# Query and key weights of an mLSTM head multiplied into one block projection, and the first head's row terms fed by two early loads

## The reference, cut to what matters

```
q = _headwise(xc, w_q)          # each group of 4 channels times its own 4 x 4 block
k = _headwise(xc, w_k)
v = _headwise(xm, w_v)
...
s = einsum('bhtd,bhsd->bhts', qc, kc) * exp(d - m_t)         # scores between tokens t and s
num = a * einsum('bhtd,bhdv->bhtv', qc, C) + einsum('bhts,bhsv->bhtv', s, vc)
...
wk = kc * exp(g - m_new)
C_new = decay * C + einsum('bhsd,bhsv->bhdv', wk, vc)         # memory update
```

## Time and profile before

| | |
|---|---|
| median of three runs | 3260.99 us (3259.97 to 3262.92) |
| profiled execution, its own time | 3259.83 us |
| its span, first to last instruction | 3258.1 us |
| mean granted TensorE clock | 0.988 of full |
| PE busy | 3145.2 us, 97% |
| DVE, ACT, POOL busy | 1394.8, 823.0, 811.0 us |
| phase B, all four heads | from about 1636 us to about 2270 us of the span |

### The profile page before, as it was taken

The page is one execution under the profiler, slowest core; times in us unless marked ns, Lnnn a source line. Parts: engine busy times, 40 slices in busy tenths (PEclk is TensorE's granted clock), DMA queues, the critical chain, the costliest instruction groups (busy, mean ns, idle before and its releaser), DMA issues.

```text
span 3258.1 us, 51785 instructions
## 1 busy us (share of the span) xinstructions
PE 3145.2 (97%) x20960; PEld 2903.3 (89%) x20960; DVE 1394.8 (43%) x2066; ACT 823.0 (25%) x1545; POOL 811.0 (25%) x520
## 2 busy tenths in 40 slices
PE   7999899999999999999989999998999999999997
PEld 7777689999999998999967877777998999999996
DVE  2000445333333354433448484858326433333335
ACT  4110523111111124111144444444106111111113
POOL 2112033333233332333201010102322423333320
PEclk9999999999999999999999999999999999999999
DMA  7455311111111113333245454627510111111111
GB/s 219 119 126 125 104 52 47 46 45 45 39 52 39 52 35 128 108 111 118 86 171 206 171 209 158 233 108 275 178 47 27 59 46 52 45 45 45 45 39 54
DMA packets 275662, 318.28 MB, mean 98 GB/s; under 512 B 23565, under 2 KB 215309, under 8 KB 274298
## 3 DMA queue, kind: packets, MB, share of 16 engines
q1 hardware_dynamic: 255265, 250.27, 24.8%
q10 hardware_dynamic: 12960, 40.04, 3.2%
q0 software_dynamic: 7296, 25.96, 2.3%
HBM read 224.88 MB, written 92.19 MB: 97 GB/s over the span
## 4 chain that ended last, share of the span: by engine, by line
PE 82%; DVE 8%; ACT 5%; issue 3%; DMA 1%; POOL 0%; SPq 0%; another core or an unknown queue 0%; ACTq 0%; DVEq 0%; POOLq 0%
PE ps L379 23%; PE ps L380 22%; PE ps L381 22%; PE ps L1934 3%; PE ps L1127 1%; ACT X L462 1%; PE ps L1087 1%; PE ps L1065 1%; PE ps L1096 1%; PE ps L1097 1%; PE ps L1098 1%; DVE CT L1474 1%; PE ps L756 1%; PE ps L400 1%; DVE RST L1613 1%
## 5 line engine op out<-in xcount | busy, mean ns | idle before, releaser
L379 PE MATMUL ps<-AH,WH 128*128 128x352 f32 x3072 | 999.9, 325 | 11.2 <-DVE AL L2400 6.3
L380 PE MATMUL ps<-AL,WH 128*128 128x352 f32 x3072 | 985.7, 321 | 0.0
L381 PE MATMUL ps<-AH,WL 128*128 128x352 f32 x3072 | 985.6, 321 | 0.0
L366 POOL TENSOR_SCALAR WH<-RAW 128x1024 fp32r<-128x1024 f32 x200 | 231.6, 1158 | 1713.0 <-PEq L386 1474.9
L379 PEld LDWEIGHTS ps<-AH,WH 128*128 128x128 f32 x3072 | 577.2, 188 | 36.4 <-issue 22.4
L380 PEld LDWEIGHTS ps<-AL,WH 128*128 128x128 f32 x3072 | 578.6, 188 | 1.0
L381 PEld LDWEIGHTS ps<-AH,WL 128*128 128x128 f32 x3072 | 577.0, 188 | 0.0
L368 POOL TENSOR_TENSOR WL<-RAW,WH 128x1024 fp32r<-128x1024 f32 x200 | 503.9, 2519 | 16.7
L379 PE MATMUL ps<-HH,WH 128*128 128x352 f32 x1536 | 498.4, 324 | 0.0
L380 PE MATMUL ps<-HL,WH 128*128 128x352 f32 x1536 | 492.3, 321 | 0.0
L381 PE MATMUL ps<-HH,WL 128*128 128x352 f32 x1536 | 492.0, 320 | 0.0
(11 more groups left out here) (302 smaller groups left out, 3528.9 us busy)
## 6 DMA issues: line engine op xcount, KB each, us to landing
RAW<-in_ffn_w SPq DMA_DIRECT2D x128, 512.0 KB, 3.8
CT<-in_state_mlstm_C SPq DMA_DIRECT2D x32, 1024.0 KB, 5.6
out_C_s<-CT SPq DMA_DIRECT2D x32, 1024.0 KB, 6.2
RAW<-in_ml_w_in SPq DMA_DIRECT2D x32, 512.0 KB, 3.9
RAW<-in_conv_w_pw SPq DMA_DIRECT2D x24, 512.0 KB, 8.9
STK<-u_scratch SPq DMA_DIRECT2D x48, 190.0 KB, 4.1
xc_scratch<-XC ACTq DMA_DIRECT2D x16, 528.0 KB, 2.7
so_scratch<-SO ACTq DMA_DIRECT2D x16, 528.0 KB, 3.7
```

The costliest lines, as they stand in the source:

```text
L366: pool.tensor_scalar(WH[:, k % 4], RAW[:, k % 2], 1.0, 0.0, ALU.mult, ALU.add).then_inc(w_hi, 1)
L379: pe.matmul(ps[:, bank, 0:CW], wh[:, k, cols], hi[:, k, cs], start=(k == 0), stop=False)
L380: pe.matmul(ps[:, bank, 0:CW], wh[:, k, cols], lo[:, k, cs], start=False, stop=False)
L381: mm = pe.matmul(ps[:, bank, 0:CW], wl[:, k, cols], hi[:, k, cs], start=False, stop=(k == nk - 1))
```

## The change

What it does:

- The score is q·k, with q and k both block-wise products of the same `xc`. Instead of making both, one block projection with `M` = Wq·Wkᵀ (4 x 4 per group, scaled) gives `QT`, and the score product reads `xc` itself (`XCH`) in place of `KH`. 12 products and 12 copies per head go. `XCH` becomes two buffers in turn (`XCH`, `XCH2`), the second in the place of `KH`.
- `merged_weights` makes `M` on DVE after the first block of the first MLP, from four added loads of `w_k` (`WKR`) that SP issues before the loads of that MLP.
- The decode tokens still need the true query: `query_weights` makes a fourth set of block weights `BQ` on DVE at the start of `phase_b_dve`, and PE makes 4 products of 32 columns with it. They stand after the 12 projections and before `head_mean(END)` and the tokens. `QZ` is now made from PSUM, after `ROWB` has come; PE's prompt memory waits for it, since it writes the same bank.
- `row_terms` is split. The part that makes `BT` reads a new small tile `RT` with the 9 numbers per head that it needs, loaded for all heads by two loads. SP issues them before it waits for ACT's exponentials. The rest (`RD`, `DDR`) becomes `diagonal_terms`, done between two steps of the `WKL` loop.
- `row_exps` moves: it stood ahead of the 8 `VH` copies of head 0 and now stands after the third. The transposes of `CR` (`row_columns`) move from after token 8 to after token 5. The rows are stored in three pieces instead of one; the third waits for the exponentials, and `ROWB` is loaded after all three.
- In heads 1 to 3, `finish`, `gain`, `inverse` and `normalise` of the head before move to later places among the tokens, and the token stage's banks are used in another order.

The diff, cut to its core:

```diff
-            for x in range(24):
-                m, dt, c = x // 12, x // 3 % 4, x % 3
+            for x in range(12):
+                dt, c = x // 3, x % 3
...
-                pe.matmul(ps[:, QKB[x % 6], 0:CW], BD[:, m, dt], XCH[:, dt, ch[c]], start=True, stop=True).then_inc(qk_mm, 1)
+                pe.matmul(ps[:, QKB[x % 6], 0:CW], BD[:, 0, dt], xch(h)[:, dt, ch[c]], start=True, stop=True).then_inc(qk_mm, 1)
...
+            pe.wait_ge(qk_ev, 12 * h + 7)
+            pe.wait_ge(bd_done, 2 * h + 2)
+            for dt in range(VT):
+                mm = pe.matmul(ps[:, 3, dt * NDEC:(dt + 1) * NDEC], BQ[:, dt], xch(h)[:, dt, SEQ:TOK], start=True, stop=True, skip_group_check=True)
+            mm.then_inc(qk_mm, 1)
+            if not first:
+                head_mean(pe, h - 1, END)
...
-                if first and x == 8:
+                if first and x == 5:
                     row_columns(pe)
...
-            pe.wait_ge(qk_ev, 24 * h + 24)
+            pe.wait_ge(qk_ev, 12 * h + 12)
+            pe.wait_ge(qa_done, h + 1)
...
-                    mm = pe.matmul(ps[:, 3 + q % 2, o_:256], KH[:, dt, i * P:(i + 1) * P], QT[:, dt, tc * 256 + o_:tc * 256 + 256],
+                    mm = pe.matmul(ps[:, 3 + q % 2, o_:256], xch(h)[:, dt, i * P:(i + 1) * P], QT[:, dt, tc * 256 + o_:tc * 256 + 256],
...
-            if first:
-                row_exps()
...
             for t in range(NB):
+                if first and t == 3:
+                    row_exps()
...
+            query_weights(dve, h)
+            if not first:
+                center(dve, h - 1, DEC)
+                row_terms()
+                sum_tiles(dve, h - 1, DEC, 2)
+                sum_tiles(dve, h - 1, END, 1)
...
                 for t in range(9):
+                    if first and t == 6:
+                        columns(dve)
+                        row_terms()
...
+            dve.wait_ge(ld_row, 16 * h + 48)
+            dve.wait_ge(qk_mm, 13 * h + 13)
...
             for i in range(9):
+                if i == 2:
+                    diagonal_terms()
+                    if not first:
+                        finish(dve, h - 1, DEC)
...
+        def query_weights(dve, h):
+
+            wait(dve, den_mm, 4 * h)
+            dve.tensor_tensor(BQ[:].rearrange("p v (g o) -> p v g o", o=4), WROW[:, 0, bass.ds(4 * h, 4)].unsqueeze(2).to_broadcast([P, VT, 32, 4]),
+                              bdm[:].unsqueeze(1).unsqueeze(3).to_broadcast([P, VT, 32, 4]), ALU.mult).then_inc(bd_done, 1)
...
+            for i in range(4):
+                sp.dma_start(WKR[i:P:4].rearrange("p t i o -> p t (i o)"), wk).then_inc(s_wif, 16)
...
+            sp.wait_ge(gv, GV_END - 2)
+            sp.dma_start(ROWS[:, 0:TOK], RP[:, 0:TOK]).then_inc(rs_out, 16)
+            sp.dma_start(ROWS[:, RW - NB:RW], RP[:, RW - NB:RW]).then_inc(rs_out, 16)
+            sp.wait_ge(rs_out, 32)
+            sp.dma_start(RT[:, :, 0:NB], ROWS[:, RW - NB:RW].unsqueeze(0).to_broadcast([P, HEADS, NB])).then_inc(ld_row, 16)
+            sp.dma_start(RT[:, :, NB:], ROWS[:, SEQ - 1:SEQ].unsqueeze(0).to_broadcast([P, HEADS, 1]), allow_slow_non_contiguous=True).then_inc(ld_row, 16)
             sp.wait_ge(gv, GV_END)
             sp.wait_ge(ga_, GA_END)
-            sp.dma_start(ROWS, RP[:]).then_inc(rs_out, 16)
+            sp.dma_start(ROWS[:, TOK:RW - NB], RP[:, TOK:RW - NB]).then_inc(rs_out, 16)
```

More of the change, by code:

```diff
@@ L1279, in phase_b_act @@
                 act.wait_ge(e_g, 2)
[L1280 to L1284, removed]
+            for x in range(12):
+                dt, c = x // 3, x % 3
+                act.wait_ge(qk_mm, 13 * h + x + 1)
+                act.copy(QT[:, dt, ch[c]], ps[:, QKB[x % 6], 0:CW]).then_inc(qk_ev, 1)
                 if not first and x == 4:
                     square(act, h - 1, DEC)
[L1287 to L1290, removed]
+            if not first:
+                root(act, h - 1, DEC)
             if first:
-                row_exps()
                 act.wait_ge(x_spill, 16)
@@ L1300, in phase_b_act @@
                     square(act, h - 1, END)
+                if not first and t == 3:
+                    gain(act, h - 1, DEC)
                 if not first and t == 7:
@@ L1303, in phase_b_act @@
             if first:
-                act.wait_ge(rs_out, 16)
+                act.wait_ge(rs_out, 48)
                 act.wait_ge(d_out, 16 * 7)
             act.wait_ge(bt_done, 8 * h + 8)
-            act.activation(WS[:], BT[:, NB - 1], ACT.Exp, bias=ROWB[:, SEQ - 1:SEQ]).then_inc(ws_done, 1)
+            act.activation(WS[:], BT[:, NB - 1], ACT.Exp, bias=RT[:, h, NB:]).then_inc(ws_done, 1)
             act.wait_ge(ws_done, h + 1)
@@ L1378, in phase_b_dve @@
         def phase_b_dve(dve, h, first):
[L1379 to L1384, removed]
-                finish(dve, h - 1, DEC)
             def row_terms():
-                dve.wait_ge(ld_row, 16 * h + 16)
+                dve.wait_ge(ld_row, 32)
                 wait(dve, dexp, NS * h)
@@ L1409, in value_parts @@
                         dve.tensor_tensor(VL[:, t], ps[:, token_bank(t), :], VH[:, t].bitcast(F32), ALU.subtract).then_inc(tok_ev, 1)
+                        if not first and t == 0:
+                            inverse(dve, h - 1, DEC)
+                            normalise(dve, h - 1, DEC)
                         if not first and t == 1:
@@ L1442, in phase_b_dve @@
             for i in range(9):
+                if i == 2:
+                    diagonal_terms()
+                    if not first:
+                        finish(dve, h - 1, DEC)
+                if i == 7:
+                    dve.wait_ge(qa_done, h + 1)
+                    dve.wait_ge(e_nrm, 1)
+                    wait(dve, o_out[1], 16 * 2 * h)
+                    for dt in range(VT):
+                        ins = dve.tensor_tensor(mdec(QN[:, dt], DEC_T), own_columns(dt), NT[:, :, hd(h, dt)].to_broadcast([P, DEC_B, DEC_T]), ALU.mult)
+                    ins.then_inc(qn_done, 1)
                 dve.wait_ge(tok_mm, 18 * h + 10 + i)
@@ L2426, in _ @@
             ffn_dve(dve, 0, 0, first=True)
+            merged_weights(dve)
             with dve.Fori(1, FB - 1) as b:
```

79 lines of the change are left out of this document (44 added, 35 removed).

## The result

The changed kernel took 3243.9 us (median of five runs, 3242.96 to 3244.68) against 3260.99 us for the kernel before; the ratio is 0.9947, with a 95% interval of 0.9933 to 0.9962. That is 17 us faster, where 16.2 were predicted. The profiled execution has a span of 3242.2 us (before 3258.1) and a mean granted clock of 0.987 (before 0.988).

What follows compares the result with a forecast made beforehand. PE, busy in 97% of the span, was taken as the bound. Heads 1 to 3 gain 19.2 us and head 0 loses 3.0, so 16.2 off 3260.99 gives 3244.8, rounded 3245; range 3237 to 3254.

Steps and rivals of the forecast that it cites:

- Heads 1 to 3, 6.4 us each: First projection to first prompt memory product: 12 fewer products save 7.26 us, less 0.9 and 0.1, plus 0.2; 19.2 us together.
- Head 0, a loss of 3.0 us: Head start: PE idles 9.1 us for `BQ`, half clock follows, exponentials and `ROWB` come late; 3 won to 8 lost.
- Prompt memory and scores, nothing: Behind each head's first prompt memory product: nothing gets shorter; the score product's new operand costs the same.
- `ROWB` and `XO`, 0.6 us: Head 0: POOL's four `XO` loads run beside `ROWB` and delay it, 0 to 4 us possible, 0.6 taken.
- Rival B: Head 0 loses 8 us because `ROWB` lands 12 us after its issue; total 3250 us; chance 0.15.
- the prediction's case of an even interleaving: Head 0: 2 MB of `XO` interleaved evenly with `ROWB` puts its landing nearer 11.8 than 7.5 us; head 0 loses 7.
- Rival A: Head 0 wins 2 us if the wait for `ROWB` does not bind; total 3240 us; chance 0.12.
- Rival C: Tokens of heads 1 to 3 take half back through added ACT and DVE work; 3.2 us per head, 3254; chance 0.11.
- Rival D: Pauses in the tokens halve PE's clock for prompt memory of heads 1 to 3; 8.3 us slower, 3269; chance 0.04.
- The front and the back, nothing: Outside the head starts: `w_k` loads hidden by POOL's 37.11 us idle, `merged_weights` about 1 us beside PE, last head 0.

Runs made afterwards that it cites:

- putting the products back: Changed kernel with 12 products of 352 columns, whose results nobody reads, put back on PE in each of heads 1 to 3: 3261.81 us.
- early `BQ`: Changed kernel with DVE making head 0's `BQ` ahead of the chain of row steps instead of behind it: 3234.58 us.
- exponentials first: Changed kernel with ACT's three exponentials of head 0 back ahead of the eight `VH` copies, `BQ` still behind the row steps: 3234.57 us.
- fastest version: Changed kernel with head 0's `BQ` made ahead of the row steps and decode queries copied out of PSUM before `WKL`: 3230.19 us.
- filled version: Changed kernel with 14 products of 352 columns, read by nobody, put into PE's 9.1 us wait for `BQ` in head 0: 3238.6 us.

## Why the prediction was right, and where its errors cancelled

The time was right within 1.1 us, and the named mechanisms are there. That the sum came within 1.1 us was luck, because terms were off in ways that cancelled: of 16.2 us forecast, heads 1 to 3 gave 3.2 more, head 0 took 2.6 more, its memory 0.8, the score stages gave 4.2, front and back took 4.3, which makes the 15.9 of the profiles.

- *Heads 1 to 3, 6.4 us each.* Mechanism shown by putting the products back. The forecast's own terms add up to 6.46, written as 6.4. The step of the projections was right: 6.26 us forecast, 6.21 measured in head 2; the four small products took 0.81 us (0.9 forecast). Mis-sized was the token stage: 0.2 us of gain forecast, 0.68 measured, because the first of the two waits shrank from 0.53 to 0.15 us and the 32 records ahead of it took 3.73 us for 4.04. The rest of the surplus lies in the kernel before, where head 2 alone had stood for all three: head 1's first six products took 1.4 us longer than head 2's, at half clock, and head 3 took 0.34 us longer, with one wait for `VL` more in its tokens (0.39 us). Three times 0.48, 1.43 and 0.34 are the 3.2 us by which 22.4 exceeds 19.2.
- *Head 0, a loss of 3.0 us.* The chain was the forecast one, link by link: 9.11 us idle (9.1 forecast), half clock behind it, exponentials, stores, `ROWB`, `QZ`, `WKL`; `BT` ready long before `ROWB`. The loss was 5.6. The step that failed is the pace behind the idle stretch. The prediction took 8.25 us from `BQ` being ready to the exponentials' end, with one of three tokens at full clock and 0.55 us for the small products, less than even the 0.9 it gave them in the other heads. It took 10.7: all three tokens ran at half clock (third copy 6.1 us after the tokens' start, 4.75 forecast) and the small products took 1.70 us. That is 2.5 of the 2.6 us missed; with the stretch filled the same path took 7.37 us, so the clock explains all but 0.3 of it against the 7.05 that the prediction gave for a full clock. Two smaller errors cancelled: from the exponentials' end to the issue of `ROWB` it took 1.91 us (2.58 forecast), from there to `QZ` 8.85 (8.1 forecast). The section of the Trainium skill cited there (TensorE: Matmul & The Clock Gate, "What's actually happening") had the direction right; the error was in how long the lower level was taken to last.
- *Prompt memory and scores, nothing.* Wrong both ways: head 0's memory lost 0.8 us to the half clock behind the longer wait, the score stages gained 4.2 with no instruction of PE less. Of these, 2.1 us are the seam of heads 0 and 1, which the kernel before showed twice at 97.0 and the changed kernel twice at 94.9; why the clock falls longer there in one kernel than in the other stays open.
- *`ROWB` and `XO`, 0.6 us.* Rival B's 12 us landing did not come: 8.85 us from issue to `QZ`, 7.5 + 0.6 forecast. The Trainium skill (DMA: Bandwidth & Descriptors, "Issuing engines are not separate DMA queues") says that transfers of different engines interleave on the same DMA engines, and the prediction's case of an even interleaving, near 11.8 us, rests on that. It did not come, though POOL issued `XO` 4.5 us behind `ROWB`, when little had moved: in the four us from 1670 to 1674 the traffic was 112, 26, 0 and 69 GB/s, 0.2 MB of the 1.08 MB that `ROWB` has. Holding `XO` back changed 0.2 to 0.8 us; why so little stays open.
- *Rival A* fell by `QZ` and the late exponentials; without them head 0 wins not 2 but 6.2 us (30.20 against 36.41). *Rival C* fell: PE's waits in a head's tokens are 1.1 us together. *Rival D* fell: the prompt memories of heads 1 to 3 are 31.9 us before and after.
- *The front and the back, nothing.* The first MLP's panels were not late: POOL's idle stretch at its start is 37.15 us, before 37.11, and phase B's later start is within scatter. Behind phase B the changed kernel's two profiles have 991.5 and 990.7 us, the kernel before 989.0 and 988.1. Variants with the same back part lie between 988.7 and 991.4, so part or all may be scatter; the rest stays open.

## What to carry to other kernels

Before an operand is made new on an engine, look at what stands in that engine's queue at that moment: a 0.7 us instruction at the head of a stage waited behind 12 us of steps that had nothing to do with it, and made ahead of them it kept PE waiting no more. When a consumer of a late load only shares a bank with something urgent, copy its input out of the bank (0.27 us here) and let it wait alone. A load sent early can hold up what its queue issues next: with the early `BQ` the two small ones cost `ROWB` 1.55 us. And price an idle stretch of PE with its echo: what followed it on PE here ran at the lower clock for 4.5 to 7.4 us, and all that hung on it was late by the difference.

## What the runs showed of the hardware

The idle stretch of 9.1 us was followed by about 7.4 us at 0.50 of the clock while PE was busy without a break (PE went on at 1656.92; 0.50 in all of 1656 to 1664, 0.91 in the next 2 us). The length is not fixed: behind the same stretch it was 6.8 us in the second profile of the changed kernel and 4.5 us with the exponentials first. When the stretch was filled with useless products, the clock stayed at 1.00 through the exponentials and the kernel got 4.7 us faster. Behind waits of 4.31 and 5.60 us (changed kernel, early `BQ`) the clock was 0.50 again; behind waits of 0.86 us (fastest version) and 1.24 us (heads 1 to 3) the next products ran at full rate. A short wait is no safe sign: in the filled version the clock fell to 0.50 behind waits of 1.00 and 0.57 us, and in the kernel before behind one of 2.12 us (PE went on at 1657.93, and the clock was 0.50 in 1660 to 1662).

The clock also fell at the seams of heads, where PE showed no pause in the record (4.00 us busy of 4.00): 3 to 4 us of it at some seams, about 10 at the seam of heads 0 and 1 in the kernel before. In the 8 us ahead of them PE's record has short pauses (3.44 to 3.53 us busy in one stretch of 4 us), but it has them as well ahead of head 3 of the changed kernel, where no dip followed, so their cause stays open. The dips move with the kernel: in two profiles each of the kernel before and of the changed kernel the score stages agree within 0.1 us, while the variants differ from them at one seam or another. The differences that they make in a stretch are 1.4 to 2.1 us each, and so a change of 2 us read from one stretch need not show in the whole time.
